# Layer 0's expert layers in one phase: the context's picks gathered row by row and summed on VectorE, the latents dense in plain fp32

## The chip, the core and the metric

The kernel runs on one core of one Trainium2 chip. The time is the device time of one execution, in microseconds (us). Engines: TensorE (PE, with its weight loads PEld), VectorE (DVE), ScalarE (ACT), GpSimd (POOL) and SyncE (SP), which issues most DMAs.

## The reference, cut to what matters

Two models run one after the other. The second has two layers over two streams of 256 tokens with 1024 features: the latents and the context. Each layer ends with an expert layer ("PEER") for each stream; the context needs it in layer 0 only, so there are three in all: context of layer 0, latents of layer 0, latents of layer 1. All arithmetic is fp32.

```python
def peer_ffn(h, wq, sub_keys, eu, ev):                  # for each block of 128 tokens t
    q = (t @ wq).reshape(TOKEN_BLOCK, PEER_HEADS, 2, PEER_DK // 2)          # 8 heads, two halves of 64
    s = jnp.einsum("thpd,hpnd->thpn", q, sub_keys)                          # 128 keys for each half
    st, it = lax.top_k(s, PEER_TOPK)                                        # 16 of each half
    cand = (st[:, :, 0, :, None] + st[:, :, 1, None, :]).reshape(TOKEN_BLOCK, PEER_HEADS, 256)
    cidx = (it[:, :, 0, :, None] * N_KEYS + it[:, :, 1, None, :]).reshape(...)
    best, pos = lax.top_k(cand, PEER_TOPK)                                  # 16 experts of 16384
    e = jnp.take_along_axis(cidx, pos, axis=-1)
    g = jax.nn.softmax(best, axis=-1)
    act = jax.nn.gelu(jnp.einsum("thkd,td->thk", jnp.take(eu, e, axis=0), t))
    return jnp.einsum("thk,thkd->td", g * act, jnp.take(ev, e, axis=0))
```

So every token picks 8 x 16 = 128 experts. Each expert has a row of 1024 in `eu` (64 MB in all) and one in `ev` (64 MB).

## The kernel before, in words

All three expert layers are computed densely: instead of fetching the picked rows, the kernel streams all of `peer_u` and all of `peer_v` past the 256 tokens of one stream, in 128 blocks of 128 x 1024 each (512 KB), and multiplies with a matrix of weights that is zero for what wasn't picked. One such pass is one phase of the loop `for s in streams`; for layer 0 it runs twice, context (s = 0) first, then latents (s = 1), and each pass streams both tables again.

A pass has these parts. **Queries**: 8 blocks of `w_q2`, evacuated into `qT`. **Scores** for 2 blocks of 128 tokens, then on VectorE the **search** for the 16 + 16 keys and the 16 pairs (`top16`: MAX8, FIND_INDEX8, MATCH_REPLACE8, and three wide steps for each side), one for each block of tokens. **Up**: 128 blocks of `peer_u`; `up(c)` on TensorE fills a bank of four, ScalarE applies GELU into row c of `S`. **Build**: from what was found (turned by `turn_found`), for each token a 128 x 128 matrix of weights, as a product of two one-hot matrices, four tokens (a quad) at a time, 64 quads; `gate` on VectorE multiplies them into `S`. These run between the ups. **Down**: 128 blocks of `peer_v`; `down(c)` adds into four banks of PSUM for the whole pass.

Products are not done in plain fp32 but in three products of split operands (fp32r): each streamed block gets a high part (ScalarE, `ring_hi`, 4 slots) and a low part (GpSimd or VectorE, in place in `ring`, 6 slots), and the moving side is split likewise. So an up block is 8 x 3 matmuls of 256 columns and a down block 4 x 3 of 512 columns. `product` (L275) is the plain form, 8 matmuls of fp32, and is used for the output projections.

SP issues the blocks in the order of the list `order`, 6 slots ahead of `blocks_done`. Engines have their own program each, in order, with semaphores between them. After each pass a short phase turns the sums back and adds them to `X`; much of the next pass's or of layer 1's preparation (norm, split, two query or projection blocks) is put into the end of the pass and into this phase.

Of the kernel before, what the change touches and what calls it, by code (L numbers as in the profile page):

```python
# [8 lines left out]
F32 = mybir.dt.float32  # L9
# [6 lines left out]
P = 128  # L16
D = 1024
# [159 lines left out]
def build(nc, x, smalls, consts, mix_tables, tables, axial, w_in1, w_lru, w_br, w_o1, w_f1, w_f2, ada, w_in2,  # L177
          w_out2, w_q2, keys2, peer_u, peer_v, lam, out):
    ctx = ExitStack()
    with ctx:  # L180
# [16 lines left out]
        ring_hi = ctx.enter_context(nc.sbuf_tensor("ring_hi", [P, NH, SLOT], F32R))  # L197
# [30 lines left out]
        for l in range(LAYERS):  # L228
# [3 lines left out]
            for _ in range(2 if l == 0 else 1):  # L232
                order += [(w_q2[l], i) for i in range(8)]
                order += [(peer_u[l], i) for i in range(NK)]
                order += [(peer_v[l], i) for i in range(NK)]
# [917 lines left out]
        def output_both(mix, sq, rs, mod):  # L1153
# [3 lines left out]
            with Phase("by_dve", "c_sq", "c_sum", "c_root", "c_chain", "c_normed", "c_high", "first_hi", "first_lo",  # L1157
                       "x_normed") as (
                    block, by_dve, c_sq, c_sum, c_root, c_chain, c_normed, c_high, first_hi, first_lo, x_normed):
# [5 lines left out]
                def _(pe):  # L1165
                    for i, (s, d) in enumerate(steps):
# [3 lines left out]
                        if 1 <= i <= KT:  # L1170
                            pe.wait_ge(c_sq, i)
                            mm = pe.matmul(bank[7][:, 0:T], ones[:, :], sq[:, i - 1, :], start=(i == 1), stop=(i == KT))
                            if i == KT:
                                mm.then_inc(c_sum, 1)

                @block.scalar
                def _(act):
# [5 lines left out]
                    for kt in range(KT):  # L1183
                        act.wait_ge(c_normed, kt + 1)
                        act.activation(H_r[:, kt, 1, :], H[:, kt, 0, :], ACT.Identity, bias=mod[:, 24 + kt, 0:1]).then_inc(c_high, 1)
                        if kt in (3, 5, 7):
                            high(act, n0 + 16, kt // 2 - 1, first_hi)
                    high(act, n0 + 16, NH - 1, first_hi)

                @block.vector  # L1190
                def _(dve):
# [5 lines left out]
                    for i, (s, d) in enumerate(steps):  # L1197
                        if i >= 16 - NH:
                            low(dve, n0 + 16, i - 16 + NH, first_hi, first_lo)
# [12 lines left out]
                        if 11 <= i < 15:  # L1212
                            for kt in (2 * i - 22, 2 * i - 21):
                                dve.wait_ge(c_high, kt + 1)
                                dve.scalar_tensor_tensor(H_r[:, kt, 0, :], H[:, kt, 0, :], mod[:, 24 + kt, 0:1],
                                                         H_r[:, kt, 1, :].bitcast(F32), ALU.add, ALU.subtract)
# [232 lines left out]
        for l in range(LAYERS):  # L1449
# [140 lines left out]
            with Phase("by_act", "by_dve", "padded", "tables_in", "v_tap", "a_hi", "a_soft", "v_state", "a_en",  # L1590
# [30 lines left out]
                def _(pe):  # L1621
# [158 lines left out]
                    if not last:  # L1780
# [1195 lines left out]
```

## Time and profile before

| | |
|---|---|
| median of 3 runs | 3707.51 us (3705.19 to 3710.32) |
| the profiled execution, its span | 3707.9 us |
| TensorE busy | 3622.5 us, 98% |
| VectorE busy | 2587.6 us, 70% |
| ScalarE busy | 1721.3 us, 46% |
| GpSimd busy | 756.6 us, 20% |
| DMA | 621.09 MB, 168 GB/s over the span |

Durations of single instructions come from the profiled execution. A matmul in plain fp32 stands in the profile as two records. Matmuls are pipelined, so the step from one's start to the next's is what it costs, not its duration.

### The profile page before, as it was taken

To read this page: it belongs to the slowest core of one execution; us is meant where nothing else is said; L and a number is where in the kernel's file an instruction comes from. 1 tells how busy PE (TensorE), PEld (TensorE's weight loads), DVE (VectorE), ACT (ScalarE), POOL (GpSimd) and SP (SyncE) were. 2 spreads that over 40 slices of the span, in tenths; PEclk is the share of its full clock that TensorE was granted. 3 is DMA by queue.
4 is the path that set the end of the run, shared out by engine and by line. 5 is a ranking of instruction groups with operands and counts; after the bars stand their busy time and mean duration, and the time that the engine had idled before them with its cause. 6 is when DMAs were issued, how large, how long until landed. Compare 5 with 4: busy or idle time off the path is not lost. (4 is left out here: it accounts for less than half of the span.)

```text
span 3707.9 us, 66781 instructions
## 1 busy us (share of the span) xinstructions
PE 3622.5 (98%) x24114; PEld 3268.6 (88%) x24114; DVE 2587.6 (70%) x4881; ACT 1721.3 (46%) x3076; POOL 756.6 (20%) x302
## 2 busy tenths in 40 slices
PE   9999999999899999999999999999999999999998
PEld 8788899976799999888899999888777999998887
DVE  7552757587469888556578898556586698995555
ACT  4344345443345444555455444555443554444554
POOL 5555046000078000000086000000000680000000
PEclk9999999999899999999999999999999999999999
DMA  7767855421255444555555444555432454445554
GB/s 268 235 217 263 277 171 184 142 86 52 78 173 176 148 147 144 192 191 185 188 174 171 147 145 154 193 185 193 158 98 68 160 176 147 148 146 190 192 193 142
DMA packets 175143, 621.09 MB, mean 168 GB/s; under 512 B 19376, under 2 KB 25136, under 8 KB 174896
## 3 DMA queue, kind: packets, MB, share of 16 engines
q1 hardware_dynamic: 172192, 615.35, 49.7%
q8 instruction: 163, 2.67, 0.3%
q10 hardware_dynamic: 2704, 2.38, 0.2%
q14 instruction: 84, 0.69, 0.1%
HBM read 614.51 MB, written 1.05 MB: 166 GB/s over the span
## 5 line engine op out<-in xcount | busy, mean ns | idle before, releaser
L2441 ACT ACTIVATE ring_hi<-ring 128x1024 fp32r<-128x1024 f32 x786 | 832.4, 1059 | 507.0 <-PE bank L2370 503.2
L2313 PE MATMUL bank<-H_r,ring_hi 128*128 128x256 f32 x3232 | 932.0, 288 | 8.7 <-POOL ring_r L2298 6.5
L2315 PE MATMUL bank<-H_r,ring_r 128*128 128x256 f32 x3232 | 914.0, 283 | 0.0
L2314 PE MATMUL bank<-H_r,ring_hi 128*128 128x256 f32 x3232 | 913.8, 283 | 0.0
L290 POOL TENSOR_TENSOR ring_r<-ring,ring_hi 128x1024 fp32r<-128x1024 f32 x131 | 317.0, 2421 | 1643.7 <-ACT ring_hi L284 1643.7
L2313 PEld LDWEIGHTS bank<-H_r,ring_hi 128*128 128x128 f32 x3232 | 619.0, 192 | 11.4 <-ACT arena L2446 4.4
L2314 PEld LDWEIGHTS bank<-H_r,ring_hi 128*128 128x128 f32 x3232 | 619.7, 192 | 0.0
L2315 PEld LDWEIGHTS bank<-H_r,ring_r 128*128 128x128 f32 x3232 | 618.8, 191 | 0.0
L2298 POOL TENSOR_TENSOR ring_r<-ring,ring_hi 128x1024 fp32r<-128x1024 f32 x156 | 432.2, 2801 | 554.1 <-ACT ring_hi L2441 554.1
L2366 PE MATMUL bank<-ring_hi,w_high 128*128 128x512 f32 x1536 | 476.6, 391 | 1.8 <-DVE ring_r L2684 1.8
L2684 DVE TENSOR_TENSOR ring_r<-ring,ring_hi 128x1024 fp32r<-128x1024 f32 x390 | 474.6, 1218 | 2.5 <-ACT ring_hi L2441 2.5
L2368 PE MATMUL bank<-ring_r,w_high 128*128 128x512 f32 x1536 | 473.2, 389 | 0.0
L2370 PE MATMUL bank<-ring_hi,w_low 128*128 128x512 f32 x1536 | 473.1, 389 | 0.0
L2677 DVE TENSOR_TENSOR w_low<-arena,w_high 128x256 fp32r<-128x256 f32 x384 | 163.4, 425 | 426.8 <-ACT w_high L2518 426.7
L284 ACT ACTIVATE ring_hi<-ring 128x1024 fp32r<-128x1024 f32 x237 | 249.7, 1057 | 298.0 <-PE bank L302 248.5
L2366 PEld LDWEIGHTS bank<-ring_hi,w_high 128*128 128x128 f32 x1536 | 288.1, 188 | 61.7 <-DVE ring_r L2684 2.4
L2368 PEld LDWEIGHTS bank<-ring_r,w_high 128*128 128x128 f32 x1536 | 288.3, 188 | 60.4
L2370 PEld LDWEIGHTS bank<-ring_hi,w_low 128*128 128x128 f32 x1536 | 288.3, 188 | 60.1
L2669 DVE TENSOR_TENSOR ring_r<-ring,ring_hi 128x1024 fp32r<-128x1024 f32 x240 | 294.1, 1226 | 39.1 <-ACT ring_hi L2441 39.1
L300 PE MATMUL bank<-H_r,ring_hi 128*128 128x256 f32 x1056 | 307.1, 291 | 3.4 <-PEq L318 1.8
L301 PE MATMUL bank<-H_r,ring_hi 128*128 128x256 f32 x1056 | 298.7, 283 | 0.0
L302 PE MATMUL bank<-H_r,ring_r 128*128 128x256 f32 x1056 | 298.5, 283 | 0.0
(446 smaller groups left out, 5833.9 us busy)
## 6 DMA issues: line engine op xcount, KB each, us to landing
ring<-in_peer_u SPq DMA_DIRECT2D x384, 512.0 KB, 3.2
ring<-in_peer_v SPq DMA_DIRECT2D x384, 512.0 KB, 3.3
ring<-in_w_in SPq DMA_DIRECT2D x135, 512.0 KB, 3.6
arena<-in_ada SPq DMA_DIRECT2D x96, 512.0 KB, 5.6
ring<-in_w_f SPq DMA_DIRECT2D x72, 512.0 KB, 3.5
ring<-in_w_br SPq DMA_DIRECT2D x24, 512.0 KB, 4.7
ring<-in_w_out SPq DMA_DIRECT2D x24, 512.0 KB, 3.2
ring<-in_w_q SPq DMA_DIRECT2D x24, 512.0 KB, 3.3
```

The costliest lines, as they stand in the source:

```text
L290: eng.tensor_tensor(ring_lo[:, slot, :], ring[:, slot, :], ring_hi[:, m % NH, :].bitcast(F32), ALU.subtract).then_inc(lows, 1)
L300: pe.matmul(o, hi[:, k], x_hi(kt), start=(kt == 0), stop=False)
L301: pe.matmul(o, hi[:, k], x_lo(kt), start=False, stop=False)
L2298: pool.tensor_tensor(ring_lo[:, slot, :], ring[:, slot, :], ring_hi[:, m % NH, :].bitcast(F32), ALU.subtract).then_inc(p_lo, 1)
L2313: pe.matmul(o, hi[:, k], x_hi_[:, kt, :], start=(kt == 0), stop=False)
L2314: pe.matmul(o, hi[:, k], x_lo_[:, kt, :], start=False, stop=False)
L2315: mm = pe.matmul(o, lo[:, k], x_hi_[:, kt, :], start=False, stop=(kt == KT - 1))
L2366: pe.matmul(bank[2 * t + e][:, :], w_hi, hi[:, v], start=start, stop=False)
L2368: pe.matmul(bank[2 * t + e][:, :], w_hi, lo[:, v], start=False, stop=False)
L2370: mm = pe.matmul(bank[2 * t + e][:, :], w_lo, hi[:, v], start=False, stop=stop)
L2441: act.activation(ring_hi[:, m % NH, :], ring[:, (n0 + m) % NS, :], ACT.Copy).then_inc(a_hi, 1)
L2684: dve.tensor_tensor(ring_lo[:, slot, :], ring[:, slot, :], ring_hi[:, m % NH, :].bitcast(F32), ALU.subtract).then_inc(v_lo, 1)
```

## The change

Layer 0's two passes become one phase (`if not last:`), layer 1's pass stays as it was. In the new phase:

- The streams are no longer computed alike. The latents are dense as before, over one stream of `peer_u` and `peer_v`, but in plain fp32: `up` is `product`, `down` four matmuls of 512 columns for each block. No high and low parts are made, and `ring_hi` is used as `G`, four slots for gathered rows.
- The context's experts are gathered. For each block n of 128 tokens and each of its 128 picks, GpSimd issues one indirect DMA that fetches for each of the 128 tokens (one on each partition) the row of `eu` that it picked, 4 KB each, 512 KB in all, and likewise for `ev`: 2 x 2 x 128 = 512 gathers. VectorE's `spend()` uses each: for `eu` a multiply and sum over the row (`tensor_tensor_reduce`), for `ev` a scaled add into the sum (`scalar_tensor_tensor`, each waiting for the last). The tables in rows (`u_rows`, `v_rows`) are new inputs.
- Four searches follow each other, two for the context, two for the latents; from the second on, `tick` puts a `spend()` after each 1.45 us of search work, up to the 128th.
- The one-hot matrices on the side of the columns are made by GpSimd (`hit_keys`), between gathers. The 64 builds and gates no longer run between the ups, but all after them; one `spend()` is put beside each gate. Then come the downs, and the rest of the steps.
- The temporaries of the search lie in `S` from row `FREE` = 82 on, so GELUs from block 82 wait until what was found is kept.
- What was prepared ahead for the next pass or layer (norm, split, first query and projection blocks) goes: the output phase does the context's norm and the first high and low parts itself, and layer 1 computes all its context blocks.

```diff
+                with Phase("keys_in", ...):
+                    def _(pool):
+                        def gather(j):
+                            n, k = divmod(j, 2 * PICKS)
+                            rows = u_rows if k < PICKS else v_rows
+                            c = n * PICKS + k % PICKS
+                            if k == 0:
+                                pool.wait_ge(v_idx, n + 1)
+                            if j >= NH:
+                                pool.wait_ge(spent, j - NH + 1)
+                            pool.indirect_dma_start(
+                                G[:, j % NH, :], None, rows,
+                                bass.IndirectOffsetOnAxis(ap=idx_u[:, c:c + 1], axis=0)).then_inc(g_in[j % NH], 16)
+                        def hit_keys(q):
+                            if q >= 2:
+                                pool.wait_ge(g_ps, q - 1)
+                            for u in range(4):
+                                t = 4 * q + u
+                                ins = pool.tensor_scalar(hotB[:, q % 2, u, :], cc("iota"), cols_[:, t:t + 1], wts[:, t:t + 1],
+                                                         ALU.is_equal, ALU.mult)
+                            ins.then_inc(p_col, 1)
+                        for j in range(BEFORE):
+                            gather(j)
+                        pool.wait_ge(a_t, TT)
+                        hit_keys(0)
+                        hit_keys(1)
+                        for j in range(BEFORE, BEFORE + NH):
+                            gather(j)
+                        for q in range(QUADS):
+                            if q + 2 < QUADS:
+                                hit_keys(q + 2)
+                            gather(BEFORE + NH + q)
+                        for j in range(BEFORE + NH + QUADS, STEPS):
+                            gather(j)
...
+                        def up(c):
+                            if c < 4:
+                                pe.wait_ge(by_q, c + 13)
+                            else:
+                                pe.wait_ge(a_gelu, c - 3)
+                            product(pe, n0 + u0 + c, bank[4 + c % 4][:, 0:T], lambda kt: H[:, kt, 1, :])
...
+                        def down(c):
+                            arrived(pe, n0 + v0 + c)
+                            for t in range(TT):
+                                for e in range(2):
+                                    mm = pe.matmul(bank[2 * t + e][:, :], S[:, c, t * P:(t + 1) * P],
+                                                   ring[:, (n0 + v0 + c) % NS, e * 512:(e + 1) * 512],
+                                                   start=(c == 0), stop=(c == NK - 1))
+                            mm.then_inc(blocks_done, 1)
...
+                        for c in range(NK):
+                            up(c)
+                            if c == 3:
+                                scores(2)
+                            if c == 14:
+                                scores(3)
+                            if c == FREE + 3:
+                                turn_found(0)
+                                turn_found(1)
+                        pe.wait_ge(a_t, TT)
+                        for q in range(QUADS):
+                            build(q)
+                        pe.wait_ge(v_g, QUADS)
+                        for c in range(NK):
+                            down(c)
...
+                        def spend():
...
+                            dve.wait_ge(g_in[j % NH], 16 * (j // NH + 1))
+                            if k < PICKS:
+                                ins = dve.tensor_tensor_reduce(rows, rows, tokens(n), 1.0, 0.0, ALU.mult, ALU.add,
+                                                               act_[:, c:c + 1])
+                            elif k == PICKS:
+                                ins = dve.tensor_scalar(tokens(n), rows, act_[:, c:c + 1], None, ALU.mult)
+                            else:
+                                dve.wait_ge(spent, j)
+                                ins = dve.scalar_tensor_tensor(tokens(n), rows, act_[:, c:c + 1], tokens(n), ALU.mult, ALU.add)
+                            ins.then_inc(spent, 1)
+                            step[0] += 1
+                        def tick(us, until=PICKS):
+                            credit[0] += us
+                            while credit[0] >= 1.45:
+                                credit[0] -= 1.45
+                                if step[0] < until:
+                                    spend()
...
+                        for n in range(2 * TT):
+                            search(n)
+                        while step[0] < PICKS:
+                            spend()
+                        shares(2 * TT - 1)
+                        while step[0] < BEFORE:
+                            spend()
+                        dve.wait_ge(a_t, TT)
+                        hit_rows(0)
+                        hit_rows(1)
+                        dve.wait_ge(a_gelu, NK)
+                        for q in range(QUADS):
+                            gate(q)
+                            if q + 2 < QUADS:
+                                hit_rows(q + 2)
+                            spend()
+                        while step[0] < STEPS:
+                            spend()
...
-                    if not last:
-                        for b in range(ctx_blocks):
-                            for kt in range(KT):
-                                step(b, 0, kt)
+                    for b in range(ctx_blocks):
+                        for kt in range(KT):
+                            step(b, 0, kt)
```

`PICKS` is 128, `STEPS` 512, `BEFORE` 178, `QUADS` 64, `NH` 4, `NS` 6. `gate(q)` is one multiply over 128 x 512, and `hit_rows(q)` one comparison over 128 x 512.

## Rows read from the trace of the kernel before

**Rows 1.** The page: instructions over the span, and the main DMA queue.
```profile
PE 3622.5 (98%) x24114; PEld 3268.6 (88%) x24114; DVE 2587.6 (70%) x4881; ACT 1721.3 (46%) x3076; POOL 756.6 (20%) x302
...
q1 hardware_dynamic: 172192, 615.35, 49.7%
```

**Rows 2.** Windows (busy us, count, clock, DMA share, GB/s): layer 0's passes, their parts.
```profile
core 0: us, PE busy (x) PEld busy (x) DVE busy (x) ACT busy (x) POOL busy (x), PEclk, DMA share, GB/s
1028.90:1485.90 457.00, 454.27 (x3846) 453.06 (x3846) 386.48 (x832) 210.08 (x433) 144.21 (x52) 1.00 0.47 158
1485.90:1839.10 353.20, 352.35 (x1552) 291.26 (x1552) 209.41 (x275) 181.42 (x272) 0.00 (x0) 1.00 0.58 190
1839.10:1849.70 10.60, 9.54 (x79) 9.37 (x80) 3.50 (x8) 5.56 (x9) 3.04 (x2) 1.00 0.23 63
1849.70:2299.20 449.50, 446.72 (x3786) 445.52 (x3784) 386.54 (x832) 207.61 (x430) 143.28 (x52) 1.00 0.48 160
2299.20:2652.40 353.20, 352.34 (x1552) 291.24 (x1552) 209.34 (x275) 181.50 (x273) 0.00 (x0) 1.00 0.57 190
2652.40:2669.00 16.60, 11.32 (x81) 10.53 (x81) 6.52 (x13) 7.02 (x16) 5.73 (x6) 0.94 0.26 90
```

**Rows 3.** Timeline of PE (start, us, line, count): ups, build, plain fp32, scores, turns.
```profile
1003.39 24.34 PE L275 MATMUL bank<-arena,ring 128*128 128x256 f32 x112
...
1054.96 2.06 PE L2323 MATMUL bank<-arena 64*128 64x128 f32 x32
...
1431.34 1.06 PE L2352 MATMUL bank<-arena 128*128 128x128 f32 x8
1432.15 0.36 PE L2313 MATMUL bank<-H_r,ring_hi 128*128 128x256 f32 x1
...
1435.11 1.05 PE L2352 MATMUL bank<-arena 128*128 128x128 f32 x8
...
2655.51 1.03 PE L2817 MATMUL bank<-CS,arena 128*128 128x128 f32 x8
```

**Rows 4.** Timeline of DVE: the first search's start, its wide steps, the second's start.
```profile
1058.66 3.19 DVE L2570 MAX8 arena<-arena 128x8 f32<-128x128 f32 x16 [30.11 <-ACT arena L2452]
...
1095.65 2.27 DVE L2622 COPY arena<-arena 128x8 f32<-128x8 f32 x1
...
1098.56 2.38 DVE L2627 CAST arena<-arena 128x256 f32<-128x256 uint32 x1
1100.97 2.29 DVE L2630 TENSOR_TENSOR arena<-arena,CS 128x2048 f32<-128x2048 f32 x1
1103.30 4.38 DVE L2632 TENSOR_TENSOR arena<-arena 128x2048 f32<-128x2048 f32 x1
1107.71 2.29 DVE L2633 TENSOR_REDUCE arena<-arena 128x128 f32<-128x2048 f32 x1
1110.03 4.44 DVE L2630 TENSOR_TENSOR arena<-arena,CS 128x2048 f32<-128x2048 f32 x1
...
1121.24 0.87 DVE L2570 MAX8 arena<-arena 128x8 f32<-128x128 f32 x4
```

**Rows 5.** Groups of instructions by line and shape (busy us, mean ns of one).
```profile
L2684 DVE TENSOR_TENSOR ring_r<-ring,ring_hi 128x1024 fp32r<-128x1024 f32 x390 | 474.6, 1218 | 2.5 <-ACT ring_hi L2441 2.5
...
L2640 DVE TENSOR_TENSOR arena<-CS,arena 128x512 f32<-128x512 f32 x192 | 131.3, 684 | 6.3 <-ACT SM L2463 6.3
...
L2024 DVE SCALAR_TENSOR_TENSOR arena<-arena,SM 128x512 f32<-128x512 f32 x60 | 41.9, 743 | 0.0
...
L2657 DVE TENSOR_TENSOR arena<-arena,bank 128x504 f32<-128x504 f32 x3 | 2.0, 679 | 7.8 <-PE bank L2352 7.8
...
L2024 DVE SCALAR_TENSOR_TENSOR arena<-arena,SM 128x256 f32<-128x256 f32 x60 | 26.3, 477 | 0.0
...
L2298 POOL TENSOR_TENSOR ring_r<-ring,ring_hi 128x1024 fp32r<-128x1024 f32 x156 | 432.2, 2801 | 554.1 <-ACT ring_hi L2441 554.1
L290 POOL TENSOR_TENSOR ring_r<-ring,ring_hi 128x1024 fp32r<-128x1024 f32 x131 | 317.0, 2421 | 1643.7 <-ACT ring_hi L284 1643.7
```

**Rows 6.** The blocks of peer_v: SP's issue (min/median/max ns), and time to landing.
```profile
L254 SPq DMA_DIRECT2D ring<-in_peer_v x378: 332/333/343, 1467.6 to 3669.3; - x189
...
DMA to landing us min/median/max: 3.0/3.3/4.8
```

**Rows 7.** Windows as in rows 2: the busiest DMA stretch, and three with a lower clock.
```profile
45.00:55.00 10.00, 8.90 (x68) 6.61 (x67) 9.50 (x20) 4.40 (x8) 7.35 (x4) 1.00 1.03 415
...
950.00:960.00 10.00, 5.28 (x22) 4.11 (x21) 8.94 (x16) 5.74 (x16) 0.00 (x0) 0.67 0.00 0
960.00:970.00 10.00, 6.81 (x24) 5.73 (x24) 7.67 (x12) 3.49 (x5) 0.00 (x0) 0.50 0.01 2
970.00:980.00 10.00, 10.00 (x46) 8.71 (x46) 3.19 (x9) 0.83 (x2) 0.00 (x0) 0.97 0.30 105
```

More of the change, by code:

```diff
@@ L233, in build @@
                 order += [(w_q2[l], i) for i in range(8)]
-                order += [(peer_u[l], i) for i in range(NK)]
-                order += [(peer_v[l], i) for i in range(NK)]
+            order += [(peer_u[l], i) for i in range(NK)]
+            order += [(peer_v[l], i) for i in range(NK)]
         issued = [0]
@@ L1182, in _ @@
                     act.activation(rs, bank[7][:, 0:T], ACT.Sqrt, bias=eps[:, 0:1]).then_inc(c_root, 1)
-                    for kt in range(KT):
[L1184 to L1188, printed above, removed]
+                    for d in range(KT):
+                        if 2 <= d < 6:
+                            for kt in (2 * d - 4, 2 * d - 3):
+                                act.wait_ge(c_normed, kt + 1)
+                                act.activation(H[:, kt, 0, :], H[:, kt, 0, :], ACT.Identity, bias=mod[:, 24 + kt, 0:1])
+                        act.wait_ge(by_dve, KT + d + 1)
+                        act.activation(sq[:, d, :], X[:, d, 1, :], ACT.Square, scale=D ** -0.5).then_inc(l_sq, 1)
+                    act.wait_ge(l_sum, 1)
+                    act.activation(NR[:, 0:T], bank[6][:, 0:T], ACT.Sqrt, bias=eps[:, 0:1])
                 @block.vector
@@ L2264, in build @@
                 u0, v0 = 8, 8 + NK
-                done_q = 2 if s and not last else 0
                 C0, G0, QUADS = 48, 50, T // 4
@@ L2555, in _ @@
                             weights(2 + c)
-                            if c + NH < NK or ahead and c + NH < NK + NH - 2:
+                            if c + NH < NK:
                                 high(v0 + NH + c)
-                        if ahead:
-                            high(v0 + NK + NH - 2)
-                        if last:
-                            act.activation(eps[:, 5:6], eps[:, 0:1], ACT.Sqrt)
+                        act.activation(eps[:, 5:6], eps[:, 0:1], ACT.Sqrt)
                     @block.vector
@@ L2741, in _ @@
                             low(c)
-                        if ahead:
-                            for c in range(NK, NK + NH - 1):
-                                low(c)
                 used[0] += 8 + 2 * NK
                 y_tok = flat[:, 116 * T:116 * T + TT * D].rearrange("p (t d) -> p t d", t=TT)
-                early_q, y_banks = (2, 2) if s == 0 else (0, 4)
                 y_sq = flat[:, 72 * T:80 * T].rearrange("p (k t) -> p k t", t=T)
-                n0 = used[0]
-                with Phase("a_y", "t_ps", "v_x", "first_hi", "first_lo", "y_squares") as (
-                        block, a_y, t_ps, v_x, first_hi, first_lo, y_squares):
+                with Phase("a_y", "t_ps", "v_x", "y_squares") as (block, a_y, t_ps, v_x, y_squares):
                     @block.sync
@@ L2828, in _ @@
+                        for kt in range(KT):
+                            pe.wait_ge(y_squares, kt + 1)
+                            pe.matmul(bank[4][:, 0:T], ones[:, :], y_sq[:, kt, :], start=(kt == 0), stop=(kt == KT - 1))
                     @block.vector
```

544 lines of the change are left out of this document (399 added, 145 removed).

## The prediction, made before the changed kernel was run

> **What bounds the kernel now.** I read the page first: TensorE is busy 98% of the span and the 16 DMA engines half of it [rows 1]. Then windows over layer 0's expert layers, from the first query's start at 1028.9 us to layer 1's first product at 2669.0: 1640.1 us, in which TensorE never rests for more than a phase boundary, at full clock in the passes [rows 2]. So here a us of TensorE is a us of the kernel, as long as nothing else becomes later than it. VectorE (387 of 450 us) is next, DMA works at 158 to 190 GB/s. The timeline of TensorE gives the pace of each product [rows 3]: a pass is 136 up-like blocks, 64 builds and 128 downs; builds step by 3.77 us with one up each (1435.11 - 1431.34), of which the build is 0.81 (1432.15 - 1431.34) and the up 2.96 with its edge; a down block is 353.2 / 128 = 2.76 us [rows 2]. The span of the profiled execution, 3707.9, is within 0.4 us of the median; the sum is made against it, and 0.2% (7 us) is about what a measurement can tell from no change.
>
> **TensorE's work after.** Plain fp32 costs 24.34 / 7 = 3.45 us for a block of 8 matmuls of 256 columns [rows 3]. A down block has as many columns (4 x 512 against 8 x 256), so I take 3.45 too (no clean row for 512; columns are what is paid, 0% to 5% more). Each dense block gets dearer by 0.5 to 0.7 us, but there is one pass, not two: 16 queries, 128 ups, 128 downs at 3.45 are 938 us, builds 52, scores and turns about 15: 1005 us instead of 1627. That is the gain, if the rest can hide in it. ScalarE only keeps GELU (one per 3.45 us) and is out of the way. What replaces the context's pass is 512 gathers of 512 KB, 268 MB beside the 134 MB of the one dense pass: 402 MB, where two passes took 268.
>
> **Cost of one step.** On VectorE: multiply and sum over 128x1024 as the subtraction of that size, 1.22 us; the scaled add, by the slope from 256 to 512 columns (0.477, 0.743), 1.28; I take 1.27 with the wait [rows 5]. The gather's issue on GpSimd has no row. Bounds: SP's issue 0.33 us [rows 6] and GpSimd's own subtraction over 128x1024, 2.4 to 2.8 [rows 5]; 128 addresses are far less work than 131072 elements but more than a hardware issue: I take 1.2. Landing 3.3 us as for a plain block of 512 KB [rows 6]. A slot of `G` is then taken for 1.2 + 3.3 + 1.3 = 5.8 us, and with 4 slots a step takes 1.45 to 1.5 us (1.23 with 0.33 for the issue; 2.8 where GpSimd itself is the bound). That is without company. While TensorE eats a block in 3.45 us the stream takes 524 KB / 3.45 = 152 GB/s. What DMA can do: 415 GB/s in the busiest stretch [rows 7]; bytes over busy time of the main queue give 615 / (0.497 x 3708) = 334 [rows 1]. Between these I take 380: 228 are left for gathers, 2.3 us a step (1.99 and 2.88 at the ends).
>
> The Trainium skill (DMA: Bandwidth & Descriptors, Specifications) gives about 358 GB/s for HBM reads of a core and 435 for the fabric; the trace has 415, above the first. By 358 a step beside the stream would take 2.55 us and the sum would be about 30 us longer.
>
> **The new phase, in us from the first query.**
> 1. 8 context queries 27.6, 16 turns 2.1, their copies 2.1, scores 2.1 (x32 records in 2.06 [rows 3]), copies 2: the first search starts at 36 (before: 29.8).
> 2. A search took 62.6 us (1058.66 to 1121.24), of which 10.6 are five wide or copying steps that took about 2.1 more than their kind, 4.38 against 2.29, while GpSimd was subtracting [rows 4]. GpSimd has no long reads now: 52. Indices are there at 88.
> 3. Three more searches, 156, with 32 steps each (46 us of ticks / 1.45) at 1.27: 122. The spacing of steps is 2.9 us, no faster than what DMA gives. Shares 1: 367. Then the steps to the 128th, 32 x 2.0 = 64: 431.
> 4. TensorE meanwhile: second queries and scores to 64, ups from there at 3.45. At up 85 it turns what was found, at about 366: it must wait until 434. This stall of some 65 us is new; the ups' end is 434 + 42 x 3.45 = 579. The 50 steps up to `BEFORE` fit beside it (115 of 145).
> 5. 64 quads, now alone. VectorE: gate 0.69, comparison 0.68, step 1.27, together 2.65 [rows 5]. GpSimd: four comparisons of 128 columns at 0.35 (2.42 / 8 and an edge) and a gather, 2.6. Rows 4 show that both hold each other up when both read; 3.2 (2.65 to 4.2): 205, end 784. A build (0.81) hides in it at half clock too; the clock did fall to 1.2 GHz (0.50) where TensorE was busy 5 to 7 of 10 us and was back in the next window [rows 7].
> 6. Downs 442 us, with 270 steps left. Beside the stream 442 / 2.3 = 192 of them, then 78 x 1.5 = 117: 559, end 1343. Not TensorE but the gathers end last (507 at 415 GB/s, 626 at 334).
> 7. Output: before, 16.6 us to layer 1's first product. Twice the adds on VectorE (8 x 0.4), the context's square sum, root, reciprocal, scale and split no longer ahead: about 12 more, 28.6. Two context blocks in layer 1 (5.8 us) partly hide in its first waits: 3. End 1375.
>
> The unrolled loops cost nothing in the sum: instructions are fetched beside matmuls of 0.4 us; the cover is gone only in the gates. 1640 - 1375 = 265 saved: 3708 - 265 = **3443 us**. Its own range, from the ends of steps 5 and 6, is 3370 to 3570.
>
> **Rivals.**
> *A, DMA gives its best* (0.17). 415 GB/s, 1.99 us beside the stream, 1.45 alone, quads at 2.65: 413 for the found, 561, 731, 1243, end 1272: 3340. For it: the measured 415 [rows 7]. Against it: that stretch was large plain DMAs from one queue.
> *B, gathers keep one pace of about 2.5 us everywhere* (0.20), because GpSimd's issue takes that long or is held up by VectorE. With a pace c the phase is 88 + 278 + 1 + 32c + 148 + 64(c + 1.4) + 270c + 32 = 637 + 366c; at 2.5 it is 1552, 88 saved: 3620. For it: VectorE's steps read two tiles of SBUF, 1.27 of each 1.5 us, and rows 4 show the COPY of 8 columns at 2.27 us and wide steps doubled beside GpSimd. Against: all these are beside reads of 2.4 us.
> The Trainium skill states this as a rule (SBUF — State Buffer, Who interferes with whom): a VectorE instruction with two SBUF inputs and a GpSimd instruction that reads SBUF exclude each other. By it the indices' reading would wait, the writing of descriptors not; rows 4 agree for the first, no row has the second.
> *C, slower* (0.13). The same mechanism from its point of decision: 637 + 366c = 1640 at c = 2.74 us. The place is the tail, where 270 steps then take 740 us against 442 of downs. At c = 3.0 (random rows of 4 KB, or an issue above GpSimd's own 2.8) the searches stretch too and the end is 1745: 105 slower, 3813.
> *Likeliest* (0.50): as summed, 3443.
>
> **How the numbers follow.** The range reaches from A's 3340 past B's 3620 to 3700 (c = 2.7), and leaves out C and a little of A. Faster: the likeliest, A and B but for its edge, 0.85; within 0.2%: c between 2.72 and 2.76, 0.02; slower: C, 0.13.
>
> **What the new profile would show.** Start of VectorE's first search at 36 us into the phase; plain blocks at 3.45 us; TensorE waiting some 65 us near up 85, more if steps are slow; quads at 3.2 us; steps in the tail at 2.3 us while downs run, with DMA near full, and 1.5 after them; TensorE idle for about 117 us at the end. If the steps keep the same pace after the last down as before it, DMA isn't the bound, and B holds. If TensorE's blocks wait for `w_ready` during the downs, the stream loses its share, and the order of step 6 is wrong though its sum may hold. The prediction is wrong above all if the issue on GpSimd is far from 1.2 us.

## The result and the profile after

| | before | after |
|---|---|---|
| median of 4 runs each, same chip | 3708.91 us | 3611.61 us (3602.36 to 3614.92) |
| ratio | | 0.9731, 95% interval 0.9716 to 0.9746 |
| profiled execution, its span | 3707.9 us | 3600.5 us (the fastest of the four) |
| DMA | 621.09 MB | 754.15 MB |

The change makes the kernel 97 us faster. The prediction was 3443 us, so 265 faster. The right sign, but little more than a third of the gain came; 3611.6 lies inside its range, in the upper third, and is close to the value of its rival B (3620), though, as will be seen, not for B's reason.

The page of the kernel after: TensorE has lost 524 us of work, and a share of the span in which it waits has appeared [rows 1].

```profile
PE 3098.8 (86%) x17340; PEld 2541.8 (71%) x17340; DVE 2341.1 (65%) x4415; ACT 1027.5 (29%) x1880; POOL 1311.0 (36%) x968
...
q1 hardware_dynamic: 135184, 480.59, 38.0%
q0 software_dynamic: 73728, 268.47, 21.1%
```

q0 is the queue of the 512 gathers, with exactly the 268 MB foreseen. Windows over the new phase, which begins with the first query at 1026.0 us (columns as in [rows 2]): searches with steps between them; TensorE waiting near up 85; the remaining ups; the gates; the downs; the steps left over; the output phase.

```profile
1120.00:1392.00 272.00, 272.00 (x1283) 239.29 (x1283) 266.75 (x810) 40.00 (x91) 111.94 (x96) 1.00 0.93 336
1392.00:1454.00 62.00, 2.28 (x12) 1.65 (x10) 40.12 (x67) 0.55 (x2) 38.26 (x33) 0.55 0.86 295
1454.00:1604.50 150.50, 147.97 (x672) 129.62 (x672) 65.36 (x53) 18.94 (x49) 62.56 (x59) 0.97 0.86 324
1604.50:1951.00 346.50, 129.01 (x515) 112.32 (x513) 170.36 (x190) 0.38 (x1) 331.41 (x311) 0.51 0.32 95
1951.00:2392.00 441.00, 441.00 (x1024) 195.09 (x1024) 247.19 (x327) 0.31 (x1) 205.99 (x197) 1.00 1.00 384
2392.00:2532.00 140.00, 0.22 (x1) 0.00 (x0) 94.24 (x74) 0.00 (x0) 84.34 (x71) 0.51 0.84 277
2532.00:2562.40 30.40, 21.46 (x118) 20.35 (x119) 22.69 (x49) 20.17 (x43) 12.65 (x9) 0.74 0.10 33
```

The fourth line is the finding of the whole case. In the gates (346.5 us) GpSimd is busy 331.41 us, VectorE 170 and TensorE 129, at half clock (0.51), while DMA idles at 0.32. No other stage has GpSimd as its bound. The groups of instructions of that stretch (busy us, mean ns of one | idle before, releaser) say with what it is busy:

```profile
L2300 POOL TENSOR_SCALAR arena<-CS,arena,SM 128x128 f32<-128x128 f32 x248 | 267.0, 1084 | 34.4 <-PE bank L2365 31.9
L2365 PE MATMUL bank<-arena 128*128 128x128 f32 x512 | 128.8, 432 | 216.7 <-issue 208.2 <-POOL arena L2300 8.5
L2499 DVE SCALAR_TENSOR_TENSOR H<-ring_hi,arena,H 128x1024 f32<-128x1024 f32 x64 | 92.2, 1441 | 0.0
L2291 POOL DMA_INDIRECT ring_hi<-in_v_rows,arena x63 | 64.5, 1023 | 10.6 <-issue 10.6
L2594 DVE TENSOR_TENSOR arena<-CS,arena 128x512 f32<-128x512 f32 x62 | 45.7, 737 | 0.0
L2600 DVE TENSOR_TENSOR arena<-arena,bank 128x512 f32<-128x512 f32 x64 | 44.0, 687 | 213.6 <-PE bank L2365 213.6
```

A comparison of 128 columns on GpSimd (L2300, `hit_keys`) takes 1.084 us in the mean, where the prediction's step 5 had 0.35. Its issue of a gather (L2291) takes 1.02, where it had 1.2. The mean hides two kinds of comparison: the median of the 248 is 0.80. VectorE's idle time is put down to TensorE's bank and TensorE's to nothing that the profile names, so groups alone would leave the chain open. The timeline of one quad closes it (start, us, engine, line, count, [idle before]):

```profile
1749.82 1.03 POOL L2291 DMA_INDIRECT ring_hi<-in_v_rows,arena  x1 [0.17 <-issue]
...
1750.89 4.29 POOL L2300 TENSOR_SCALAR arena<-CS,arena,SM 128x128 f32<-128x128 f32 x4
1751.84 0.69 DVE L2600 TENSOR_TENSOR arena<-arena,bank 128x512 f32<-128x512 f32 x1 [2.68 <-PE bank L2365]
1752.45 0.69 DVE L2594 TENSOR_TENSOR arena<-CS,arena 128x512 f32<-128x512 f32 x1
1753.05 1.48 DVE L2499 SCALAR_TENSOR_TENSOR H<-ring_hi,arena,H 128x1024 f32<-128x1024 f32 x1
1755.25 1.57 PEld L2365 LDWEIGHTS bank<-arena 128*128 128x128 f32 x7 [3.74 <-issue]
1755.28 1.62 PE L2365 MATMUL bank<-arena 128*128 128x128 f32 x6 [3.48 <-issue]
1755.35 1.03 POOL L2291 DMA_INDIRECT ring_hi<-in_v_rows,arena  x1 [0.17 <-issue]
```

GpSimd goes from gather to gather without a pause: 5.53 us for a quad (1755.35 - 1749.82) = 1.03 + 4.29 and three short gaps. TensorE's next build starts at 1755.28, 0.1 us after the fourth comparison ended (1750.89 + 4.29 = 1755.18), although VectorE had its side ready at 1753.14. So TensorE waits for GpSimd, VectorE for TensorE.

### The profile page after: what moved, and what is told of

Same layout as the page of the kernel before. It is cut to its first block and busy times, and to the rows that moved or that the text cites. A ratio compares the mean times of both kernels' runs of the same rounds, so it can differ in the third digit from the quotient of the medians.

```text
span 3600.5 us, 48258 instructions
## 1 busy us (share of the span) xinstructions
PE 3098.8 (86%) x17340; PEld 2541.8 (71%) x17340; DVE 2341.1 (65%) x4415; ACT 1027.5 (29%) x1880; POOL 1311.0 (36%) x968
## 2 busy tenths in 40 slices
DMA packets 211818, 754.15 MB, mean 209 GB/s; under 512 B 23456, under 2 KB 29216, under 8 KB 211616
## 5 line engine op out<-in xcount | busy, mean ns | idle before, releaser
L2291 POOL DMA_INDIRECT ring_hi<-in_u_rows,arena x256 | 280.5, 1096 | 712.4 <-DVE arena L2586 378.3
L275 PE MATMUL bank<-H,ring 128*128 128x256 f32 x2304 | 501.7, 381 | 5.3 <-ACT arena L2438 2.5
L275 PEld LDWEIGHTS bank<-H,ring 128*128 128x128 f32 x2304 | 439.3, 191 | 66.7 <-ACT arena L2438 2.9
L290 POOL TENSOR_TENSOR ring_r<-ring,ring_hi_r 128x1024 fp32r<-128x1024 f32 x133 | 321.3, 2417 | 358.1 <-ACT ring_hi_r L284 358.1
L2373 PE MATMUL bank<-ring,arena 128*128 128x512 f32 x1024 | 441.3, 594 | 0.8 <-DVE arena L2600 0.8
L2499 DVE SCALAR_TENSOR_TENSOR H<-ring_hi,arena,H 128x1024 f32<-128x1024 f32 x254 | 336.6, 1325 | 159.1 <-DMA ring_hi<-in_v_rows,arena 155.8
L2493 DVE CUSTOM_DVE_ANT_1 ring_hi<-ring_hi,H 128x1024 f32<-128x1024 f32 x256 | 312.8, 1224 | 154.6 <-DMA ring_hi<-in_u_rows,arena 153.4
L2291 POOL DMA_INDIRECT ring_hi<-in_v_rows,arena x256 | 281.4, 1099 | 205.3 <-DVE H L2499 167.1
L284 ACT ACTIVATE ring_hi_r<-ring 128x1024 fp32r<-128x1024 f32 x235 | 247.4, 1056 | 296.8 <-PE bank L302 246.3
L2906 ACT ACTIVATE ring_hi_r<-ring 128x1024 fp32r<-128x1024 f32 x260 | 275.4, 1059 | 167.3 <-PE bank L2844 167.1
L2787 PE MATMUL bank<-H_r,ring_hi_r 128*128 128x256 f32 x1072 | 309.1, 288 | 2.1 <-POOL ring_r L2772 2.1
L300 PE MATMUL bank<-H_r,ring_hi_r 128*128 128x256 f32 x1056 | 307.1, 291 | 3.4 <-PEq L318 1.8
L2789 PE MATMUL bank<-H_r,ring_r 128*128 128x256 f32 x1072 | 303.1, 283 | 0.0
L2788 PE MATMUL bank<-H_r,ring_hi_r 128*128 128x256 f32 x1072 | 303.1, 283 | 0.0
L301 PE MATMUL bank<-H_r,ring_hi_r 128*128 128x256 f32 x1056 | 298.7, 283 | 0.0
L302 PE MATMUL bank<-H_r,ring_r 128*128 128x256 f32 x1056 | 298.5, 283 | 0.0
L2300 POOL TENSOR_SCALAR arena<-CS,arena,SM 128x128 f32<-128x128 f32 x256 | 276.6, 1088 | 34.6 <-PE bank L2365 31.9
L2772 POOL TENSOR_TENSOR ring_r<-ring,ring_hi_r 128x1024 fp32r<-128x1024 f32 x52 | 143.9, 2792 | 225.9 <-ACT ring_hi_r L2906 225.9
```

The source lines that it names most:

```text
L275: mm = pe.matmul(out_ap, col(n, kt), rhs(kt), start=(kt == 0), stop=(kt == KT - 1))
L290: eng.tensor_tensor(ring_lo[:, slot, :], ring[:, slot, :], ring_hi[:, m % NH, :].bitcast(F32), ALU.subtract).then_inc(lows, 1)
L300: pe.matmul(o, hi[:, k], x_hi(kt), start=(kt == 0), stop=False)
L301: pe.matmul(o, hi[:, k], x_lo(kt), start=False, stop=False)
L302: mm = pe.matmul(o, lo[:, k], x_hi(kt), start=False, stop=(kt == KT - 1))
L2291: pool.indirect_dma_start(G[:, j % NH, :], None, rows, bass.IndirectOffsetOnAxis(ap=idx_u[:, c:c + 1], axis=0)).then_inc(g_in[j % NH], 16)
```

## The experiments

Each kernel was timed against the kernel before on the same chip (medians of before 3707 to 3709). "After" without more is 3611.6. The phase is measured from the first query's start, which itself lies between 1022 and 1039 us in the profiled executions.

### Is GpSimd the bound of the gates?

Half of the comparisons are left out; the second token of each pair gets its neighbour's row, so that part of the result is not computed:

```diff
-                            for u in range(4):
+                            for u in (0, 2):
```

> GpSimd makes only two of the four one-hot columns of a quad (the other two tokens of the pair use their neighbour's, so the latents' expert sum is left wrong); everything else stays. Theory G (in the gates GpSimd's own queue is the bound: a gather 1.03 us, four comparisons 4.29, 0.2 between, 5.5 us a quad): a quad takes 3.4 us, the gates 218 us instead of 346, the run about 130 us shorter than the changed kernel, near 3480. Rival P (TensorE at half clock is: build 2.05 us, then gate, then the next pair of one-hots): quads stay above 5 us, at most 30 us shorter. Rival V (the hold-up between VectorE's step and GpSimd's comparisons costs the time, not their number): between them, some 70 us.

3462.99 us, ratio 0.9337 (0.931 to 0.9363): 149 faster than after. The gates took 196 us instead of 346 and nothing else moved: first query to gates 580 (after: 579), first down to last step 583 (581). Theory G had 218 for the gates; P, with quads above 5 us, is refuted (they took 3.06), and V's 70 us are too few. The second form keeps everything computed, but takes the comparisons from GpSimd: one wide comparison of 512 columns on VectorE, and the scaling on ScalarE.

```diff
+    dve.tensor_tensor(hotB[:, q % 2, :, :], cc("iota").unsqueeze(1).to_broadcast([P, 4, P]),
+                      cols_[:, r].unsqueeze(2).to_broadcast([P, 4, P]), ALU.is_equal).then_inc(v_col, 1)
...
+    ins = act.activation(hotB[:, q % 2, u, :], hotB[:, q % 2, u, :], ACT.Copy, scale=wts[:, t:t + 1])
```

> The one-hot columns are compared on VectorE (one of 128x512, 0.68 us) and weighted on ScalarE (four of 128x128), GpSimd only gathers. Theory G: a quad is now VectorE's 0.69 + 0.68 + 0.68 + 1.3 = 3.4 to 3.6 us, gates 220 to 230 instead of 346, about 120 us shorter, near 3490. Rival P: no change in the gates, near 3610. Rival V: as G or better, since GpSimd no longer reads; VectorE's step falls from 1.47 back to 1.29 us.

3467.59 us, ratio 0.934 (0.9316 to 0.9365). The window of its gates:

```profile
1620.40:1810.70 190.30, 128.24 (x513) 111.55 (x513) 188.54 (x252) 80.27 (x252) 82.28 (x63) 0.52 0.56 170
```

190.30 us, and now VectorE is busy in 188.54 of them. So the queue on GpSimd is shown to be what cost the gates 156 us, and the next bound behind it is VectorE at 2.97 us a quad, in which it now has one comparison more. (The whole kernel gained 144: the way to the gates was 5 us longer, and the stretch from the first down to the last step 9.)

### How much of it is price, how much is contention?

No gathers between the gates' comparisons, and no step beside the gates:

```diff
-                            gather(BEFORE + NH + q)
...
-                            spend()
```

> No gathers and no steps beside the gates; the 64 steps move behind them. Theory G alone: a quad is four comparisons at 1.07, 4.5 us, gates 60 us shorter, but 64 steps at 1.9 us come back at the end, 120 us: about 60 longer, near 3670. With rival V on top: the comparisons fall to their 0.80 of the undisturbed ones, quads 3.4 us, gates 135 shorter, end 120 longer: about 15 shorter, near 3595. Rival P: gates unchanged, 120 longer, 3730.

3588.85 us, ratio 0.9676 (0.9648 to 0.9704), as G with V on top had it (near 3595). The gates fell to 205.3 us, 3.21 for a quad, and the 64 steps came back at the end:

```profile
1604.90:1810.20 205.30, 128.79 (x513) 112.15 (x511) 81.33 (x127) 0.38 (x1) 201.24 (x248) 0.51 0.01 3
1810.20:2251.80 441.60, 441.56 (x1024) 195.19 (x1024) 243.35 (x310) 0.00 (x0) 211.62 (x194) 1.00 0.99 378
2251.80:2518.80 267.00, 0.00 (x0) 0.00 (x0) 179.20 (x153) 0.31 (x1) 164.35 (x137) 0.50 0.82 275
```

GpSimd is still full (201 of 205 us): the comparisons alone, at a median of 0.790 us, are the bound. That the gates took just the 205 us of the prediction is chance. The 5.53 us of a quad are thus: 4 x 0.80 = 3.2 for the comparisons, 1.03 and gaps of 0.2 for the gather, and 1.1 for being held up. In the timeline above the quad's first two comparisons take 0.80 and 0.79 us. The other two, min/median/max ns:

```profile
L2300 POOL TENSOR_SCALAR arena<-CS,arena,SM x2: 1342/1365/1388, 1752.5 to 1753.8; 128x128 f32<-128x128 f32 x2
```

Each of them starts while a VectorE instruction with two SBUF inputs runs, and ends 0.66 us after that one's end: the third after VectorE's own comparison (1753.14 to 1753.80), the fourth after its step (1754.53 to 1755.18). Together they lost 1.15 us (2.73 - 2 x 0.79); VectorE's step, which began beside the third, lost 0.20 (1.48 against 1.28).

The Trainium skill (SBUF — State Buffer, Who interferes with whom) calls this an exclusive lock between GpSimd and VectorE instructions with two SBUF inputs. The trace agrees for GpSimd, which goes on only when VectorE's instruction has ended; for VectorE's step it doesn't, since a full wait for the third comparison would have cost 0.75 us and not 0.20.

The issue of a gather is held up in the same way. The gates don't show it, because there the issue goes out while VectorE waits for TensorE (1.03 us). After the last down it does show:

```profile
2416.14 1.28 DVE L2499 SCALAR_TENSOR_TENSOR H<-ring_hi,arena,H 128x1024 f32<-128x1024 f32 x1 [0.34 <-DMA ring_hi<-in_v_rows,arena]
2416.92 1.32 POOL L2291 DMA_INDIRECT ring_hi<-in_v_rows,arena  x1 [0.30 <-issue]
```

This issue ended 0.81 us after the step (2418.23 against 2417.42). Of the 512 issues of the kernel after, 395 met no such VectorE instruction and took 0.94 us in the median. 100 began while one was running, and all of them ended 0.81 us after it, up to 2.75 us after their own start; 17 began within 0.1 us of the start of one and were not held.

Is 0.80 us a price for columns or for instructions? Two comparisons of 256 columns instead of four of 128 (again with the neighbour's key for the second token, so that part isn't computed):

```diff
-    ins = pool.tensor_scalar(hotB[:, q % 2, u, :], cc("iota"), cols_[:, t:t + 1], wts[:, t:t + 1],
+    ins = pool.tensor_scalar(hotB[:, q % 2, u:u + 2, :], cc("iota").unsqueeze(1).to_broadcast([P, 2, P]), cols_[:, t:t + 1], ...
```

> Edit: two comparisons of 256 columns (two tokens' rows at once, with the first token's key for both) in place of four of 128 in each quad. Same columns, half the instructions; the second token of each pair gets its neighbour's key and weight, so that part of the result is left wrong and only the time counts. Theory W (the 0.80 us of a comparison is a price for each column, 6.3 ns): a comparison takes about 1.55 us, the gates stay at 346 us and the time at 3612. Theory K (it is a price for each instruction, as the 0.35 of the prediction's step 5 would be if read from wider work): the gates fall to about 196 us as where two of the four were left out, and the time to 3463. In between: fixed part f and column part from the two durations, f + 128 c = 0.80 and f + 256 c = what is measured.

3560.42 us, ratio 0.9605 (0.9586 to 0.9625), between the two theories; the gates took 294 us, 4.6 for a quad. All instructions of the line, min/median/max ns, first in the kernel after, then here:

```profile
L2300 POOL TENSOR_SCALAR arena<-CS,arena,SM x256: 780/804/2451, 1559.5 to 1946.6; 128x128 f32<-128x128 f32 x128
```
```profile
L2300 POOL TENSOR_SCALAR arena<-CS,arena,SM x128: 1207/1232/2536, 1573.6 to 1903.9; 128x256 f32<-128x256 f32 x128
```

The shortest ones give f + 128 c = 780 and f + 256 c = 1207 ns: c = 3.3 ns a column and f = 0.35 us an instruction, so both (two points, and a straight line is assumed). The prediction had divided GpSimd's subtraction of 1024 columns by eight [rows 5]; that gives 0.30 us and leaves no room for a fixed part.

### What sets the pace of the steps?

After the last down a step took 1.89 us (140 / 74), where step 6 of the prediction had 1.5. Three kernels vary slots and bytes. Gathers of half rows (256 KB each; the other half of each row is replaced by the first, so that part isn't computed):

```diff
-    G[:, j % NH, :], None, rows,
+    G[:, j % NH, 0:512], None, rows.rearrange("n (a d) -> (n a) d", a=2),
```

> Each gather fetches 2 KB of a token's row instead of 4, and VectorE reads this half twice (the context's expert sum is left wrong), so addresses, issues and steps are as many and as long, bytes half. If the DMA engines bound the steps beside the downs (384 GB/s there): the pace falls from 2.24 to about 1.6 us, all 270 steps fit beside the 441 us of downs, TensorE ends last, about 140 us shorter, near 3470. If the round trip of a slot (issue, latency, step) bounds them: pace 2.0 or more, at most 60 shorter.

Three slots:

```diff
-    if j >= NH:
-        pool.wait_ge(spent, j - NH + 1)
+    if j >= 3:
+        pool.wait_ge(spent, j - 2)
```

> Edit: three slots for gathered rows instead of four. Theory R (round trip): 7.6 / 3 = 2.52 us for a step that has nothing beside it instead of 1.89, and where weights stream beside it at least 2.5 instead of 2.24; of 197 steps beside the down products some 20 or more move behind them, and the end grows by 74 x 0.63 + 22 x 2.52 = about 100 us, and by some 40 more before the gates: 3700 to 3760. Theory B (the gathers' own rate or the DMA engines' bytes bound each stretch): three slots still hold two gathers in transit, and the time stays within 20 us of 3612.

Six slots, the fifth and sixth in the memory of the one-hot rows and used only outside the gates:

```diff
+                    free = range(4) if BEFORE <= j < BEFORE + NH + QUADS else range(6)
+                    k = min(free, key=lambda i: (last[i], i))
```

> Edit: the memory of the one-hot rows, unused outside the gates, serves as a fifth and sixth slot for gathered rows before and after the gates. Theory R (with no weights in transit a step of 1.89 us is a quarter of a slot's round trip: four slots, 7.6 us): with six slots the round trip allows 1.26 us, so VectorE's 1.285 us and a gap of 0.04 to 0.2 bind: 1.35 to 1.45 us for each of the 74 steps after the down products, which saves 33 to 40 us; beside the down products the DMA engines are full already (1.00) and nothing is won. Time 3570 to 3582. Theory B (the rate of the row gathers themselves, 279 GB/s with nothing beside them, is the bound): the pace stays at 1.89 and the time at 3612.

e4_half_rows: 3509.71 us, ratio 0.9463 (0.9433 to 0.9492). e8_three_slots: 3768.72, ratio 1.0165 (1.0138 to 1.0193), so 1.65% slower than the kernel before. e6_six_slots: 3526.81, ratio 0.9511 (0.9489 to 0.9532). From the windows, duration over number of gathers issued (beside the downs) or of steps (after them); a slot's round is that pace times the slots:

| | beside the downs | slot's round | DMA share, GB/s | after the downs | slot's round |
|---|---|---|---|---|---|
| three slots | 442 / 156 = 2.83 us | 8.5 us | 0.93, 334 | 262.4 / 115 = 2.28 us | 6.8 us |
| after: four slots | 441 / 197 = 2.24 | 9.0 | 1.00, 384 | 140 / 74 = 1.89 | 7.6 |
| six slots | 442 / 224 = 1.97 | 11.8 | 1.02, 415 | 73.9 / 49 = 1.51 | 9.0 |
| four slots, half rows | 442 / 232 = 1.91 | 7.6 | 0.86, 288 | 58.6 / 38 = 1.54 | 6.2 |

```profile
1993.80:2435.70 441.90, 441.85 (x1024) 195.27 (x1024) 193.43 (x285) 0.31 (x1) 163.96 (x156) 1.00 0.93 334
2435.70:2698.10 262.40, 0.00 (x0) 0.00 (x0) 147.82 (x115) 0.00 (x0) 116.01 (x112) 0.51 0.73 231
```
```profile
1939.70:2382.00 442.30, 442.30 (x1024) 195.45 (x1024) 280.02 (x352) 0.31 (x1) 275.56 (x224) 0.99 1.02 415
2382.00:2455.90 73.90, 0.07 (x1) 0.00 (x0) 62.15 (x49) 0.00 (x0) 51.37 (x44) 0.52 0.92 336
```

The first fence is three slots, the second six. The round trip is the bound with nothing beside the rows: from three to six slots the pace goes from 2.28 to 1.51. It is not a constant, though: it grows with what is in transit, and shrinks by 1.4 us when a row has half the bytes. What I had not expected is the first column: beside the downs the round trip counts as well, although the DMA engines of the kernel after are shown busy 1.00 of the time. With six slots they moved 415 GB/s at 1.02. So a busy share of 1.00 at 384 GB/s was not full. Whether 415 is the end, no run shows. That is why the six slots brought 85 us and not 40 (14 before the gates, where a stream runs too, 65 from the first down on), and the three slots cost 157, a little past the 150 of the expectation's end. Half the bytes gave 102 us, between what pure bytes and a pure round trip would give: both count. The expectations for three and six slots had the mechanism right and the stretch beside the stream too small.

### Do the idle 38 us and the 60 us stall matter?

VectorE did no step between its 178th (1566 us) and the end of the ups (1604), and TensorE waited 60 us near up 85.

196 gathers before the gates instead of 178:

```diff
-                BEFORE = 178
+                BEFORE = 196
```

> Edit: 196 instead of 178 gathers are issued before the gates' comparisons. In the changed kernel VectorE has done its 178th step at 1566 us and the up products end at 1604, so GpSimd and VectorE have nothing to do for the rows for about 38 us, while the steps that are left over run alone at 1.89 us each at the end. Theory Q (GpSimd's program order decides what is gathered when): 17 or 18 steps fit into the 38 us at 2.2 us each, the gates start at most 5 us later, and the end loses 18 x 1.89 = 34 us: about 3580 us, 3572 to 3592. Theory D (the DMA engines' bytes set the end, whatever the order): those 38 us were used by the layer's weights that would now come later, so the time stays within 5 us of 3612.

3593.83 us, ratio 0.9681 (0.9653 to 0.9708), 18 us faster, short of the 34. The tail after the downs did fall from 140 to 109 us, but the gates began 6 us later, counted from the first query (584.5), and took 7 us longer (353.5), because GpSimd's first eight comparisons no longer lie ahead of them.

The last tile's shares before the remaining steps of the first half:

```diff
-                        while step[0] < PICKS:
-                            spend()
                         shares(2 * TT - 1)
```

> Edit: VectorE works out the last tile's shares (for which TensorE sits 60 us) before the row steps that are left of the first half, and ScalarE's gelu of the picks is moved up to match. Theory S (the 60 us stall costs the end only what GpSimd's order lets through): the up products end at about 1544, but the gates' first comparisons wait in GpSimd's program for the 178th gather, which went out at about 1560; so the gates start about 40 us earlier and all behind them with them: about 3572 us, 3565 to 3590. Theory F (the stall is paid in full): 3552. Theory D (the DMA engines set the pace before the gates, which then start no earlier, since the rows now share the engines with weights all the time): 3600 to 3612.

3589.71 us, ratio 0.9678 (0.9649 to 0.9707), 22 us faster. The ups ended after 518 us instead of 579, so the whole stall of 60 us went, and yet the gates began only at 551: GpSimd's program puts the comparisons behind the 178th gather, and that went out at 1573. Of these 28 us 7 came back in the gates and 5 after the downs; that leaves 15 in the profiled executions, and 22 between the medians is within the noise of it. The stall was mostly covered by the gathers, as theory S had it; its size was 18 us too large, for the same eight comparisons and because the 178th gather itself came 11 us later, counted from the first query, with weights beside the rows all the way.

### Together

Both diffs of e2_keys_dve_act, the six slots, and more gathers before the gates:

```diff
-                BEFORE = 178
+                BEFORE = 202
```

> Edits together: comparisons on VectorE and scaling on ScalarE (GpSimd only gathers), six slots outside the gates, 202 gathers before the gates. From the single edits: gates 190 us instead of 346 (3468 us alone), six slots -85 us (the steps beside the down products at 1.99 us and those alone at 1.51), 24 steps moved into VectorE's 53 idle us before the gates: they save 24 x 1.5 = 36 us at the end, of which up to 10 come back as a later start of the gates. If the gains add: 3468 - 85 - 28 = 3355 us, 3340 to 3375. If the DMA engines' bytes are by then the bound from the first row to the last (they moved 415 GB/s beside the down products with six slots), the six slots and the earlier steps give together no more than the larger of them: about 3385.

3337.85 us, ratio 0.9004 (0.8989 to 0.9019): 369 us faster than the kernel before on the same chip, 274 faster than after, with everything computed. It is 2 us below the expected band, so the single gains add. Its windows from the first step to the gates, for the gates, the downs and the rest:

```profile
1125.50:1598.70 473.20, 424.89 (x1982) 372.72 (x1980) 403.28 (x956) 61.72 (x149) 241.66 (x202) 0.95 0.96 362
1598.70:1788.50 189.80, 128.60 (x512) 111.79 (x512) 187.99 (x261) 80.22 (x252) 143.10 (x63) 0.51 0.57 171
1788.50:2229.80 441.30, 441.22 (x1024) 195.12 (x1024) 280.88 (x343) 0.31 (x1) 285.62 (x225) 1.00 1.02 415
2229.80:2267.00 37.20, 0.00 (x0) 0.00 (x0) 30.93 (x25) 0.00 (x0) 21.05 (x19) 0.53 0.89 339
```

Only 25 steps are left behind the downs, and DMA is nearly full in two of the stages (0.96 and 1.02). In these gates VectorE hardly pauses, and an issue on GpSimd takes 2.27 us (143.10 / 63) instead of 0.94: had GpSimd other work there, this hold-up would count. With the shares first and `BEFORE = 178` instead:

> Edits together: comparisons on VectorE and scaling on ScalarE, six slots outside the gates, and the last tile's shares ahead of the row steps that are left, so that TensorE doesn't stall before the last up products; 178 gathers before the gates. The shares edit alone took 28 us off the way to the gates and gave back 5 in the tail and 7 in the comparisons of the first two quads, which are no longer on GpSimd here. With six slots the 178th step is done 27 us earlier than with four, so the gates can follow the up products at once: 3468 - 85 - 45 + 6 = 3344 us if all add, 3330 to 3370. If the steps before the gates now slow down because rows and weights share the engines all the way, 3370 to 3385.

3348.92 us, ratio 0.9032 (0.9008 to 0.9055): as expected, and not to be told from e9 with certainty (its runs were 3338 to 3353, those of e9 3337 to 3338). The gates begin 32 us earlier than in e9, and the 48 steps left behind the downs (71 us) take that back.

## Why the prediction was wrong, step by step

From the first query, against the steps of the new phase:

| step | predicted | measured |
|---|---|---|
| 1, first search starts | 36 | 35.5 (1061.52) |
| 2, indices there | 88 | about 88 |
| 3, 128th step | 431 | 426 |
| 4, TensorE's stall; ups end | 65; 579 | 60; 578.7 |
| 5, gates | 205 | 346.3 |
| 6, downs; rest | 442; 117 | 441; 140 |
| 7, output, and layer 1's own part | 28.6 + 3 | 22.2 + 7.4 |
| sum | 1375 | 1535.6 |

The longest wait of TensorE in that phase before the gates, of which step 4 had spoken:

```profile
PE bank L2356 <- DVE arena L2541: 59.7, 1, 59.7
```

**What was right.** The mechanism and its parts: TensorE's plain blocks at 3.45 us (441 / 128), the first search at 52.5 us without GpSimd's reads beside it (52 foreseen), the stall, the ups' end to within a microsecond, the gathers ending last, about 1.2 us or less for a gather's issue, and layer 1's extra 7.4 us instead of 3 (the part of the kernel from its first product at 2554.2 on, 1046.3 against 1038.9) balanced by a shorter output phase. Two small slips of the sum did no harm: 24.34 / 7 is 3.48 and not 3.45, and the ends given for step 6, 507 and 626, come out as 512 and 617 by its own paces.

**The step that failed is 5**, and in it above all one term: GpSimd's "four comparisons of 128 columns at 0.35 (2.42 / 8 and an edge)". Each costs 0.80 alone and 1.08 in the mean of the gates, where nearly half of them are held up. The gates came out 141 us longer than 205, which is 88% of the 161 us by which the phase's sum is off. In quads: 2.6 us were given to GpSimd, and 3.2 with the hold-up; it takes 3.2 + 1.2 = 4.4 with no contention and 5.5 with it. So of the missing 2.3 us a quad 1.8 are the price and 0.5 the hold-up. The range of that step (2.65 to 4.2) did not hold 5.5 either; its upper end had a factor for contention, and none for the price itself. The trace of before had no short GpSimd instruction that reads (the comparison's 0.35 us fixed part shows in no row of it), so the bounds should have been a fixed part of several tenths of a us for each, times 256 of them.

**Step 6 was too short by 22 us**, in its second half. 1.5 us a step assumed that a slot is free again 5.8 us after its issue began. The round took 7.6. The issue took the 1.2 us foreseen (0.94 with hold-ups). But landing was priced as for a plain block (3.3 us), where in the trace the step starts 4.4 us after the end of the issue; and 0.7 us from the end of a step to the next issue into its slot were not priced at all. The pace beside the downs, 2.24 against 2.3, agreed, but for a reason half wrong: I took it from DMA's capacity (380 GB/s, measured 384), and six slots showed that 415 were to be had.

**The rivals.** B gave nearly the right time by luck. Its mechanism, issues held up by VectorE, exists, but is far too small: 0.94 us for an issue that isn't held, 1.7 in the mean for the 100 that were, and not 2.5. The pace was not one but 2.24, 1.89 and 5.4, and B's 250 us for the gates and 675 for the rest (measured: 346 and 581) are wrong in opposite directions. C did not come about. Paces beyond its 2.74 us stand only in the kernel with three slots (2.83 beside the downs, 2.28 after them), which was slower than the kernel before; but there the slot's round sets the pace, not the issue. The test that the prediction named against B, a different pace after the last down, came out as it said.

## What to carry to other kernels

Price a short instruction as a fixed part and a part for each column, engine by engine, and before moving work to the engine that looks idle, add up its queue for one round of the loop in which it will stand: here 4 x 0.80 + 1.2 us on GpSimd against 2.05 on TensorE. A gather through few slots runs at round trip / slots, also where the DMA engines look full, and the round grows with what is in transit; count slots as well as bytes. And when the work of an in-order engine is only sequenced (gathers, then comparisons), time freed on another engine arrives only if that order lets it through.

## What the runs showed of the hardware

- A GpSimd comparison and multiplication over one input (fp32), from its two sizes (0.780 us for 128 columns, 1.207 for 256): 0.35 us and 3.3 ns for each column of 128 partitions.
- A GpSimd comparison, or issue of a gather, that starts while a VectorE instruction with two SBUF inputs runs ends 0.66 or 0.81 us after that one's end: comparisons of 0.79 us took 1.34 and 1.39, issues of 0.94 us up to 2.75, and in the gates of e9_all_202 2.27 in the mean. VectorE's step of 1.28 us grew to 1.48 in the gates.
- An indirect gather of 128 rows of 4 KB: 0.94 us of GpSimd for its issue when nothing holds it; the step that uses it starts 4.4 us after the issue's end with four slots and no stream; slots' rounds of 6.8 to 9.0 us with three to six in turn and no stream beside them, 8.5 to 11.8 with one.
- The DMA engines' busy share stood at 1.00 with 384 GB/s and at 1.02 with 415 GB/s on nearly the same mix of queues. It doesn't say how much more they can do.
- Random rows of 4 KB beside a plain stream reached the same 415 GB/s as the best stretch of plain blocks of the kernel before [rows 7]. The Trainium skill (DMA: Bandwidth & Descriptors, Specifications) has about 358 for a core, the memory's 716 divided between two cores; this kernel runs on one, and here the measurement decides: 415 over 442 us, about two thirds of it random rows (224 x 0.524 of 183 MB).
- TensorE was busy 129 of 346 us in the gates and had the lower clock there (0.51, the 1.2 GHz level), and the full one in the downs after (1.00).
